# Two FFN loops of a two-block transformer kernel: one more weight pair a turn by seven products, FFN 1's low parts two granules at a time, FFN 2's squares on ScalarE and its residual by DMAs

## The reference

```python
# block 1, D_FF = 5632
h2 = rmsnorm(x, ffn_norm_g[l])
x = x + (jax.nn.silu(h2 @ w_ffn_gate[l]) * (h2 @ w_ffn_up[l])) @ w_ffn_down[l]
# block 2, D_FF_2 = 8192
h = rms_norm(x, g_ff[l])
x = x + jnp.square(jax.nn.relu(h @ w_ff1[l])) @ w_ff2[l]
```

## Time and profile before

| | |
|---|---|
| median of three runs | 2575.62 us |
| span of the profiled execution | 2573.7 us |
| TensorE busy | 2567.3 us, 11501 matmuls |
| VectorE busy | 2015.8 us |
| ScalarE busy | 1451.4 us |
| GpSimd busy | 536.5 us |
| granted TensorE clock | 1.000 |

### The profile page before, as it was taken

How to read it: one execution, slowest core, us unless ns; L and a number is a source line. 1 busy time by engine, 2 the same in 40 slices (tenths; PEclk the granted TensorE clock), 3 DMA queues, 4 the chain that set the end, 5 groups by cost and what they waited for, 6 DMA issues and landing times.

```text
span 2573.7 us, 34186 instructions
## 1 busy us (share of the span) xinstructions
PE 2567.3 (100%) x11501; PEld 2134.4 (83%) x11501; DVE 2015.8 (78%) x2102; ACT 1451.4 (56%) x1615; POOL 536.5 (21%) x1034
## 2 busy tenths in 40 slices
PE   9999999999999999999999999999999999999999
PEld 8888888888888888888878888888888888888888
DVE  6767888666988888888886655566679988998895
ACT  5546666445565555555555557774455555555553
POOL 2212221233112112222133120003322112211121
DMA  8666666766688888888787655556666766666674
GB/s 274 210 206 212 216 197 208 255 214 209 209 238 246 245 241 244 247 242 243 240 291 216 210 183 195 174 191 211 223 202 215 231 206 218 201 220 206 206 228 154
DMA packets 291153, 564.76 MB, mean 219 GB/s; under 512 B 28512, under 2 KB 41872, under 8 KB 290544
## 3 DMA queue, kind: packets, MB, share of 16 engines
q1 hardware_dynamic: 247616, 502.25, 59.0%
q0 software_dynamic: 43264, 61.18, 10.5%
q10 hardware_dynamic: 176, 0.07, 0.0%
HBM read 503.75 MB, written 2.10 MB: 197 GB/s over the span
## 4 chain that ended last, share of the span: by engine, by line
PE 97%; DVE 1%; DMA 1%; SPq 0%; DVEq 0%; ACT 0%; issue 0%; ACTq 0%
PE pair L2491 22%; PE pair L2486 22%; PE pair L2495 22%; PE pair L2776 8%; PE aux L2776 6%; PE aux L2761 3%; PE aux L2755 3%; PE aux L2758 3%; PE pair L2758 1%; PE pair L2755 1%; PE pair L2761 1%; PE aux L2653 0%; DMA raw<-in_w_ffn_down 0%; PE aux L2648 0%; PE pair L2573 0%; PE pair L2566 0%
## 5 line engine op out<-in xcount | busy, mean ns | idle before, releaser
L845 ACT ACTIVATE w_hi<-raw 128x1024 fp32r<-128x1024 f32 (+1 forms) x786 | 818.2, 1053 | 722.1 <-PE pair L2495 571.4
L1499 DVE TENSOR_TENSOR w_lo<-raw,w_hi 128x1024 fp32r<-128x1024 f32 (+1 forms) x788 | 937.7, 1214 | 342.1 <-ACT w_hi L845 323.2
L2486 PE MATMUL pair<-w_hi,lhs_hi 128*128 128x512 f32 x1568 | 422.6, 391 | 0.8 <-ACT lhs_hi L897 0.8
L2491 PE MATMUL pair<-w_hi,lhs_lo 128*128 128x512 f32 x1568 | 419.7, 389 | 0.6 <-DVE lhs_lo L1552 0.5
L2495 PE MATMUL pair<-w_lo,lhs_hi 128*128 128x512 f32 x1568 | 419.7, 389 | 0.0
L766 POOL DMA_DIRECT2D arena<-arena x528 | 262.4, 603 | 668.9 <-DVE arena L2003 291.0
L2491 PEld LDWEIGHTS pair<-w_hi,lhs_lo 128*128 128x128 f32 x1568 | 294.2, 188 | 63.0 <-DVE lhs_lo L1552 1.4
L2495 PEld LDWEIGHTS pair<-w_lo,lhs_hi 128*128 128x128 f32 x1568 | 294.0, 188 | 62.2 <-DVE w_lo L1499 1.0
L2486 PEld LDWEIGHTS pair<-w_hi,lhs_hi 128*128 128x128 f32 x1568 | 292.2, 188 | 60.6 <-ACT lhs_hi L897 1.2
L2486 PE MATMUL pair<-w_hi,low_hi 128*128 128x512 f32 (+1 forms) x992 | 263.4, 387 | 0.0
L2491 PE MATMUL pair<-w_hi,low_lo 128*128 128x512 f32 (+1 forms) x992 | 262.0, 386 | 0.0
(11 more groups left out here) (366 smaller groups left out, 3244.1 us busy)
## 6 DMA issues: line engine op xcount, KB each, us to landing
raw<-in_w_ff SPq DMA_DIRECT2D x128, 1024.0 KB, 5.2
raw<-in_w_in SPq DMA_DIRECT2D x118, 1024.0 KB, 5.3
raw<-in_w_ffn_down SPq DMA_DIRECT2D x44, 1024.0 KB, 5.1
raw<-in_w_ffn_gate SPq DMA_DIRECT2D x80, 512.0 KB, 6.6
raw<-in_w_ffn_up SPq DMA_DIRECT2D x80, 512.0 KB, 7.5
raw<-in_w_out SPq DMA_DIRECT2D x32, 1024.0 KB, 5.7
arena<-arena POOLq DMA_DIRECT2D x840, 32.0 KB, 4.4
xres<-sums POOLq DMA_DIRECT2D x36, 512.0 KB, 9.8
```

Source lines behind the costliest of these rows:

```text
L845: nc.scalar.activation(w_hi[:, at.slot(p, k), :, 0:width], raw[:, at.raw_slot(p, k), 2 * h:2 * h + 2, 0:width], ACT.Copy).then_inc(hi_read ...
L1499: v.tensor_tensor(w_lo[:, at.slot(p, k), :, 0:n], raw[:, at.raw_slot(p, k), 2 * h:2 * h + 2, 0:n], w_hi[:, at.slot(p, k), :, 0:n].bitcast( ...
L2486: nc.tensor.matmul(ps[:, t, 0:n], hi_t[:, ch, tok], w_hi[:, s, c, 0:n], start=start and k == 0 and c == 0, stop=False)
L2491: nc.tensor.matmul(ps[:, t, 0:n], lo_t[:, ch, tok], w_hi[:, s, c, 0:n], start=False, stop=False)
```

## The change

- Which units go by seven products: 1, 3, 4, 6, 7 in FFN 1 and in FFN 2's first turn; 0, 1, 3, 4, 6, 7 in its other turns. Unit 1's sums of the tokens get buffers of their own (`one_pair`, `one_sum`, `one_hi`, `one_lo`), formed ahead of each loop by `pair_forms`; unit 0's are renamed.
- VectorE forms unit 3's sums ahead of unit 2's low parts, and the order of sums, low blocks and low sums differs a little by unit. FFN 1 has a second buffer for the high parts of the sums.
- `lo_two`: the low parts of two granules in one operation of 128x2048, for ordinary units and FFN 1's down panels.
- A `seven` unit on TensorE does the three products that need no weight sums first and frees its slots after these nine matmuls (twelve before); unit 7 then does the product with T2, which ends the second bank.
- FFN 2: ScalarE does Relu and then Square in place; VectorE's four multiplications are gone. The first three down panels are copied by ScalarE into `gates` and added to the residual by accumulating DMAs from GpSimd (`copy_part`, `add_part`); `add_x` is left for the fourth. `hid_turn` of the turn's first half moves to the start of the turn.

```diff
-SEVEN = (1, 3, 5, 7)
-FIVE = (0, 1, 3, 5, 7)
+UP1 = Turn((1, 3, 4, 6, 7), False, 0, 0)
+UP2_FIRST = Turn((1, 3, 4, 6, 7), True, 0, 0)
+UP2 = Turn((0, 1, 3, 4, 6, 7), True, -(TURNS1 + 1), 1)
...
+            def add_part(j, i):
+
+                pool.wait_ge(sums_copied, i * 3 + (COPIES1 + j + 1))
+                pool.sem_inc(moving, 1)
+                pool.dma_start(xres[:, :, j * N:(j + 1) * N], gates, accum_op=ALU.add).then_inc(parts_added, 16)
+
+            move(NB1 + T_FF2)
+            with pool.Fori(0, TURNS2 - 1) as i:
+                for n in range(2):
+                    move(i * 2 + (NB1 + T_FF2 + 1 + n))
+                for j in range(3):
+                    add_part(j, i)
+            for n in range(2):
+                move(NB1 + T_FF2 + 2 * TURNS2 - 1 + n)
+            add_part(0, TURNS2 - 1)
+            move(NB1 + T_FF2 + 2 * TURNS2 + 1)
+            add_part(1, TURNS2 - 1)
+            add_part(2, TURNS2 - 1)
...
+            def relu_squares(rows):
 
                 for t in range(TOK):
-                    nc.scalar.activation(dst[:, t, :], src[t], ACT.Relu, scale=x_inv[:, t:t + 1])
+                    nc.scalar.activation(rows[:, t, :], rows[:, t, :], ACT.Relu, scale=x_inv[:, t:t + 1])
+                act.drain()
+                nc.scalar.activation(rows, rows, ACT.Square)
                 act.drain().then_inc(act_ready, 1)
 
+            def copy_part(at, j, i):
+
+                panel_done(at, 2 + j)
+                if j == 0:
+                    act.wait_ge(flipped, i * 2 + (NB1 + T_FF2 + 3))
+                if j > 0 or not isinstance(i, int) or i > 0:
+                    act.wait_ge(parts_added, i * 48 + 16 * j)
+                nc.scalar.activation(gates, pairs[at.pair(2 + j)][:], ACT.Copy).then_inc(sums_copied, 1)
...
+            def lo_two(at, p, k):
+
+                dve.wait_ge(hi_ready, at.gran(p, k) + 2)
+                v.tensor_tensor(two_slots(w_lo, at, p, k), raw[:, at.raw_slot(p, k)],
+                                two_slots(w_hi, at, p, k).bitcast(F32), ALU.subtract).then_inc(lo_ready, 2)
...
             def block(at, i, n_aux=4):
 
-                unit_pair(at, 2, i)
-                unit_pair(at, 4, i)
+                sums_seven(at, 3, i)
+                lo_ordinary(at, 2)
+                lo_sums(3, i)
+                lo_blocks(at, 3)
+                sums_seven(at, 4, i)
+                lo_blocks(at, 4)
+                lo_sums(4, i)
                 hid_turn(i)
-                unit_pair(at, 6, i)
-                lo(at, 2, 0, 2)
+                lo_ordinary(at, 5)
+                for u in (6, 7):
+                    sums_seven(at, u, i)
+                    lo_blocks(at, u)
+                    lo_sums(u, i)
+                lo_two(at, 2, 0)
                 recombine(at, i, n_aux)
...
+            def block2(at, i, last=False, turn=UP2):
 
                 n = i + TURNS1
                 b = i * 2 + NB1
-                unit_pair(at, 2, n, False, five)
                 hid_turn(b)
-                unit_pair(at, 4, n, False, five)
-                unit_pair(at, 6, n, False, five)
+                sums_seven(at, 3, n, turn)
+                lo_ordinary(at, 2)
+                lo_sums(3, n, turn)
+                lo_blocks(at, 3)
+                sums_seven(at, 4, n, turn)
+                lo_blocks(at, 4)
+                lo_sums(4, n, turn)
+                lo_ordinary(at, 5)
+                for u in (6, 7):
+                    sums_seven(at, u, n, turn)
+                    lo_blocks(at, u)
+                    lo_sums(u, n, turn)
                 hid_turn(b + 1, 4)
                 lo(at, 2, 0, 2)
```

More of the change, by code:

```diff
@@ L27 @@
+from collections import namedtuple
 import numpy as np
@@ L476, in up_loads, with sevens, sums_free, buffer_of @@
         return i * 32 + (u // 4 * 16 + 16)
[L478 to L490, removed]
+    def sevens(i, u, turn):
+        return i * len(turn.units) + (turn.units.index(u) + turn.base)
+    def sums_free(i, u, turn):
+        return sevens(i, u, turn) + (2 if u == 1 and turn != UP2 else 1)
+    def buffer_of(u, turn):
+        b = (turn.units.index(u) + turn.odd) % 2
+        return t_sum[b], t_his[b if turn.wide else 2 * b], t_lo[b]
     def two_slots(ring, at, p, k):
@@ L1442, in block2 @@
+            def block2(at, i, last=False, turn=UP2):
                 n = i + TURNS1
                 b = i * 2 + NB1
[L1444 to L1451, removed]
+                act.wait_ge(gran_used, at.gran(0) + SPLIT)
+                hid_turn(b, 0, T_FF2 - 1)
+                hi_ordinary(at, 2, None)
+                hi_sums(3, n, turn)
+                hi_seven(at, 3, None)
+                hi_seven(at, 4, None)
+                hi_sums(4, n, turn)
+                hi_ordinary(at, 5, None)
+                hid_turn(b + 1, 4, T_FF2 - 1)
+                for u in (6, 7):
+                    hi_seven(at, u, None)
+                    hi_sums(u, n, turn)
@@ L2135, in _ @@
             lo(at, 1, 4, 6)
+            pair_forms(2, one_pair, one_sum)
             dve.wait_ge(s_hi_ready, 1)
@@ L2412, in block2 @@
                 hid_turn(b + 1, 4)
                 lo(at, 2, 0, 2)
-                recombine(at, n, 0, five)
+                if turn == UP2:
+                    dve.wait_ge(parts_added, i * 48)
+                recombine(at, n, 3, turn)
                 lo(at, 2, 2, 4)
                 dve.wait_ge(act_ready, b + 3)
-                for t in range(TOK):
-                    v.scalar_tensor_tensor(act_f[:, t, :], gates[:, 1 - t, :], x_inv[:, t:t + 1],
-                                           act_f[:, t, :], ALU.mult, ALU.mult)
@@ L2430, in block2 @@
-                if not five:
-                    first_forms()
-                lo(at, 4, 0, 4)
-                add_x(at, 3, N)
+                flip(b + (2 + T_FF2), by_chunk(gates), n_split=1)
+                lo(at, 3, 0, 4)
+                if turn == UP2_FIRST:
+                    pair_forms(0, zero_pair, zero_sum)
+                lo(at, 4, 0, 4)
+                dve.wait_ge(act_ready, b + 4)
                 flip(b + (3 + T_FF2), by_chunk(hid), n_split=1)
@@ L2742, in _, with ordinary @@
             gemm(at, 1, wide)
-            def ordinary(at, u, five=False):
+            def ordinary(at, u, turn=UP1):
                 p, k0 = unit(u)
@@ L2755, in ordinary @@
                         nc.tensor.matmul(bank[t, w], lhs_hi[:, ch, tok], w_hi[:, s, w, :],
-                                         start=c == 0 and (u == 0 or (five and u == 2 and (t, w) == (1, 0))), stop=False)
+                                         start=c == 0 and (u == 0 or (turn == UP2 and u == 2 and (t, w) == (1, 0))), stop=False)
                     for t, w, tok in parts:
```

305 lines of the change are left out of this document (167 added, 138 removed).

## The result

The changed kernel takes 2646.38 us (median of 4 runs, 2643.89 to 2647.06) against 2575.80 of the kernel before (4 runs, 2575.19 to 2576.27): ratio 1.0272, 95% interval 1.0257 to 1.0287. It is 70.6 us slower; 61.1 were forecast (2636.7 less 2575.62). Its profiled execution took 2643.89 us with a span of 2642.2, which is 68.5 us over the span before.

The account below looks back on a forecast made before the run. TensorE bounds the kernel, VectorE's chain in the units one microsecond behind. 4.3 + 9 x 2.3 + 6.9 + 6 x 3.8 + 6.4 = 61.1 us on a 2573.7 span, plus 1.9: 2636.7 us, bounds 2623 to 2650.

Parts of the forecast that it names:

- What bounds it: Whole kernel: TensorE, busy throughout, bounds it; VectorE's work in the units is only one microsecond behind.
- a second chain: VectorE's work from unit 1's low blocks to recombine's first operation; TensorE's slack 1.0 us in FFN 1, 0.8 in FFN 2.
- FFN 1's turn: Steady FFN 1 turns: first panel 43.1 us after unit 0, TensorE stalls 3.0 us, turn 64.9 us, +2.3 in each of nine.
- FFN 2's turn: Steady FFN 2 turns: first panel 43.9 us after unit 0, turn 87.6 us, +3.8 in each of six.
- if the gaps on TensorE sit elsewhere: Sign of error: TensorE idle elsewhere than, as forecast for FFN 1, before unit 7 and the first panel; no size given.
- First turns: First turn of each loop: `pair_forms` and a low part delay unit 1's low blocks; +4.3 us FFN 1, +6.9 FFN 2.
- The last turn: End of FFN 2: the next panel waits behind a ScalarE copy held by accumulating DMAs landing in 9.8 us; +6.4 us.
- The relief is worth nothing: FFN 2 behind recombine: four multiplications and three additions leaving VectorE shorten no wait that ends last; given nothing.
- The sum: Whole kernel: first, steady and last turns add 61.1 us to the span of 2573.7; runs' median 1.9 us over the span.
- moving unit 3's sums, the second buffer for high parts and the earlier release of slots I cost at nothing: FFN 1 turn: these reorder VectorE's chain, taken to have no gaps, so no cost; opening a gap would add.
- work, not order: Rival: VectorE's total work per turn decides; starting its chain 3 us earlier would bring the 11.6 us, 2566 us; chance 0.07.
- DMAs bind each turn: Rival, FFN 2 turns: accumulating DMAs landing in 13.0 us delay unit 0's blocks, 4 us each turn, 2658 us; chance 0.13.

Follow-up runs that it names:

- Experiment 1: Four idle VectorE maxima (4.2 us) added: to the kernel before, in FFN 1's units, 2597.03 us; to the changed kernel, in FFN 2's panels, 2646.20 us.
- experiment 3c: Changed kernel with GpSimd issuing the second accumulating DMA of FFN 2's last turn ahead of the last row move: 2642.50 us.
- experiment 5: Changed kernel with VectorE adding FFN 2's three residual parts, no accumulating DMAs: 2635.38 us; second kernel, also unit 1's low sums and `hid_turn` early: 2639.05 us.
- experiment 6: Changed kernel with sevens at 1, 3, 5, 7 (FFN 2 later 0, 1, 3, 5, 7), their forms and order taken back, rest kept: 2594.01 us, 1.0070 of before.
- Experiment 3a: Changed kernel with unit 1's low sums ahead of its low blocks in both loops, ScalarE's high sums earlier likewise: 2636.03 us.
- experiment 3b: Changed kernel with recombine's first operation ahead of the first panel's low parts, in FFN 2 ahead of the second `hid_turn` too: 2667.40 us.

## Why the prediction was right, point by point

*What bounds it.* Right: before the change TensorE bounded the kernel at 100% busy, with a second chain one microsecond behind, and the change put 4.75 us into that. Experiment 1 shows it without the change.

The Trainium skill ("Perfetto Trace Analysis", Identifying the Most-Contended Engine) picks the engine of highest occupancy to optimize; for TensorE it would judge by the weight loads' share or by the floating-point rate rather than by the matmuls, and the weight loads too stand highest here, at 83% beside VectorE's 78%. The runs show that this alone does not decide: with fewer matmuls on TensorE, 11450 against 11501 in the two pages of the profile, the kernel is 2.7% slower.

*FFN 1's turn.* Forecast 1.86 + 40.0 + 1.3 = 43.1; measured 1.85 + 39.86 + 1.37 = 43.08, with the stall at unit 7 and at the bank as said. The view has 1.77 and 0.43 us of idle time; counted by the starts of its matmuls TensorE is 2.9 us late in the turn, against 3.0 forecast, 2.2 of it at unit 7 and 0.7 at the bank. Turn 64.97 against 64.9.

*FFN 2's turn.* Forecast 1.5 + 41.1 + 1.3 = 43.9; measured 1.85 + 40.94 + 1.59 = 44.38. The chain had its length; its start and the end of recombine's operation were 0.3 us late each, though 0.2 of the first is the prediction's: the window of the earlier trace rows begins at 2191.25, and TensorE's first matmul of unit 0 there at 2191.02, so the start before was 1.7 us, the units 40.33 and the turn 83.99. By the sign "if the gaps on TensorE sit elsewhere" the prediction missed one: 0.6 to 0.7 us at unit 2 in each FFN 2 turn, since the hidden rows and unit 3's sums (2238.71 to 2242.91) now stand ahead of unit 2's low parts. It does not lengthen the chain. Six turns cost 25.5 where 22.8 were forecast, 1.7 of the difference a spell of reduced clock.

*First turns.* 5.1 and 6.9 against 4.3 and 6.9, and the second agreement is in part luck: FFN 2's units took 47.1 us where 47.7 were forecast, and 0.6 us more stand ahead of its unit 0. Unit 1's low blocks did come 5.1 us after unit 0 in FFN 1; the 0.8 us more in FFN 1 are ahead of unit 0, which started at 661.29 instead of 660.44: `pair_forms` delays the panel before it too.

*The last turn.* A stall of 6.4 forecast, 6.6 measured, by the steps named: the first two accumulations landed 10.3 and 9.6 us after their issue, near the 9.8 of the earlier trace rows. But 9.8 is no price for each of these DMAs: the eight of FFN 2's 21 that were issued right behind row moves landed in 9.0 to 10.3 us, the other thirteen in 5.2 to 6.8. The two that the last turn waits for are both of the first kind. What was missed is behind the stall: 2.7 us more, 2.4 of it reduced clock (twelve matmuls 0.2 us further apart). And the size of this step rests on the order that GpSimd was given too, not on the DMAs' speed alone (experiment 3c: 4.0 us instead of 6.6).

The Trainium skill ("DMA: Bandwidth & Descriptors", Anatomy of one DMA) would have them land in 3.2 us; this trace has 9.6 and 10.3 for these two, and 6.5 in the median over FFN 2.

*The relief is worth nothing.* Right: four more operations of VectorE in the panels cost a steady turn nothing (experiment 1), its additions back there 0.15 us a turn (experiment 5), and without the additional sevens the relief gained nothing (experiment 6).

*The sum.* It had 61.1 us over the span before, the trace has 68.5. The 7.4 between are reduced clock (1.7 in FFN 2's turns, most of 2.9 at the end), FFN 1's first turn (0.8), its steady turns (1.0: the panels take 21.88 instead of 21.76 us) and FFN 2's chain (1.0). The median of the runs stands 4.2 us over the profiled span, where 1.9 were taken.

*The step that failed,* though it moved no number: "moving unit 3's sums, the second buffer for high parts and the earlier release of slots I cost at nothing: they reorder a chain without gaps". There were two gates in a turn. Sevens side by side at 6 and 7 make the part behind unit 2's end nearly as long as the whole: in FFN 1 it holds the units at 42.46 with the first chain relieved, and at equal counts of sevens it costs 1.3 and 3.4 us a turn. It stayed invisible because the other chain was 0.6 us longer. `lo_two` is of the same kind: its gain of 0.07 us holds in a chain without gaps, and where VectorE waits for ScalarE, as in experiment 6, merging moved recombine back by 1.1 us.

*Rival "work, not order"* supposed that a chain begun 3 us earlier brings the 11.6 us. Experiment 3a brought 2.3 of these 3 us, and 0.6 us a turn of FFN 1 came. *Rival "DMAs bind each turn"* did not happen in the changed kernel, but in experiment 3b, by its own mechanism: there the first DMA of a steady turn landed in some 11 us. Its two slow landings in a row did not occur in a steady turn; the second took 5.2 to 6.4 us.

No version here beats the kernel before. Sevens at 0, 1, 3, 5, 7 in FFN 1, which would load VectorE in the panels and keep the alternation, were not tried.

## What to carry to other kernels

Before giving an engine at 78% more work to save the one at 100%, measure the stretch in which the work lands, from the event that releases it to the event that needs it: with one microsecond of slack there, 4.75 us of added work cost 2.4 and 4.0 us a turn although the fuller engine had less to do. Then look for a second gate behind the first, since relieving one chain only shows the next; where two kinds of work alternate, one heavier and one lighter than the other engine's pace, keep them alternating. A move off a busy engine helps only in the stretch where that engine is late, and a copy that waits for a DMA in an in-order queue holds up all that stands behind it.

## What was not expected of the hardware

The granted clock was 1.00 through the profile before. In the changed kernel's it fell at two places: around 2365 us (0.66 in the 5 us from there), and for the 5 us right behind the 6.6 us stall, rows above. Experiment 6 shows it in the same place: 0.61 and 0.71 in the two windows of 5 us in which its 7.5 us stall ends and work goes on. In experiment 5 (first kernel), without that stall, it was 1.00 from 2560 to 2600 us, yet 0.66 from 2366 to 2371, and also from 700 to 705 and from 765 to 770. So a stall of some 7 us came with 2.7 and 2.4 us beyond its length; the other dips, at no long stall, come in different turns of different kernels (in experiment 3b in every second turn of FFN 1), and what brings them stays open.
